# A sum of weight tiles made by accumulating transfers in place of VectorE adds, in a two-block transformer on one core

## The reference, cut to what matters

```
x = x + rmsnorm(m, g[1])
h = rmsnorm(x, g[2])
f = jnp.square(jax.nn.relu(h @ mlp_w1[i])) @ mlp_w2[i]     # (256,2048) @ (2048,8192), then @ (8192,2048)
x = x + rmsnorm(f, g[3])
```

## Time and profile before

| what | value |
|---|---|
| three runs | 2268.59, 2268.76, 2268.84 us (median 2268.76) |
| span of the profiled execution | 2266.9 us |
| granted TensorE clock, mean | 0.999 |
| PE busy | 2255.3 us, 99% of the span |
| DVE busy | 1675.5 us, 74% |
| ACT busy | 1332.9 us, 59% |
| moved by DMA | 542.63 MB, mean 239 GB/s |

### The profile page before, as it was taken

The page is one execution under the profiler, slowest core; times in us unless marked ns, Lnnn a source line. Parts: engine busy times, 40 slices in busy tenths (PEclk is TensorE's granted clock), DMA queues, the critical chain, the costliest instruction groups (busy, mean ns, idle before and its releaser), DMA issues.

```text
span 2266.9 us, 26633 instructions
## 1 busy us (share of the span) xinstructions
PE 2255.3 (99%) x10625; PEld 1873.7 (83%) x10625; DVE 1675.5 (74%) x2025; ACT 1332.9 (59%) x1775; POOL 104.5 (5%) x138
## 2 busy tenths in 40 slices
PE   9999999999999999999999999999999999999998
PEld 7778888888888888888888888888888888888887
DVE  6676864887788788787878788778788685456664
ACT  6455444766666666666666666666666564444443
POOL 0000000000000000000000000000000010000000
PEclk9999999999999999999999999999999999999999
DMA  9454455899998999886578999989888645643343
GB/s 358 167 174 162 164 186 186 289 291 272 287 303 265 277 292 267 283 282 236 219 281 240 287 289 261 285 281 277 270 281 258 240 152 223 244 172 149 148 163 116
DMA packets 77132, 542.63 MB, mean 239 GB/s; under 512 B 8682, under 2 KB 9013, under 8 KB 13968
## 3 DMA queue, kind: packets, MB, share of 16 engines
q1 hardware_dynamic: 61568, 429.58, 50.2%
q0 software_dynamic: 15296, 111.23, 22.7%
q10 hardware_dynamic: 144, 0.12, 0.0%
HBM read 534.60 MB, written 6.29 MB: 239 GB/s over the span
## 4 chain that ended last, share of the span: by engine, by line
PE 98%; DVE 2%; issue 0%; ACT 0%; ACTq 0%; POOLq 0%; POOL 0%
PE P L359 95%; PE P L362 3%; DVE low L626 0%; DVE R_h L614 0%; DVE R_f L611 0%; DVE R_f_r L611 0%; DVE R_g L614 0%; DVE X L614 0%; ACT R_h L502 0%; ACT EV L533 0%; DVE st L614 0%; DVE R_f L708 0%; ACT X L502 0%; DVE X L611 0%; ACTq L2710 0%
## 5 line engine op out<-in xcount | busy, mean ns | idle before, releaser
L626 DVE TENSOR_TENSOR low<-raw,hi 128x1024 fp32r<-128x1024 f32 (+3 forms) x694 | 813.4, 1200 | 290.7 <-ACT hi L507 286.4
L507 ACT ACTIVATE hi<-raw 128x1024 fp32r<-128x1024 f32 (+3 forms) x694 | 704.5, 1040 | 463.5 <-PE P L359 309.5
L359 PE MATMUL P<-hi,R_h 128*128 128x512 f32 (+2 forms) x2944 | 944.2, 392 | 0.6 <-DVE R_h L614 0.6
L359 PE MATMUL P<-hi,R_f_r 128*128 128x512 f32 x2480 | 791.4, 391 | 0.1
L359 PEld LDWEIGHTS P<-hi,R_h 128*128 128x128 f32 x2944 | 552.3, 188 | 116.4 <-issue 5.8
L359 PE MATMUL P<-low,R_h 128*128 128x512 f32 (+2 forms) x1472 | 570.2, 387 | 0.0
L359 PEld LDWEIGHTS P<-hi,R_f_r 128*128 128x128 f32 x2480 | 465.6, 188 | 96.3 <-DVE R_f_r L611 0.3
L359 PE MATMUL P<-low,R_f_r 128*128 128x512 f32 x1240 | 482.5, 389 | 0.0
L626 DVE TENSOR_TENSOR low<-R_f,hi 128x1024 fp32r<-128x1024 f32 x226 | 267.7, 1221 | 82.9 <-ACT hi L507 82.2
L359 PEld LDWEIGHTS P<-low,R_h 128*128 128x128 f32 x1472 | 276.7, 188 | 54.7 <-issue 2.6
L359 PEld LDWEIGHTS P<-low,R_f_r 128*128 128x128 f32 x1240 | 233.0, 188 | 47.1
(11 more groups left out here) (229 smaller groups left out, 1406.2 us busy)
## 6 DMA issues: line engine op xcount, KB each, us to landing
raw<-in_w_d SPq DMA_DIRECT2D x128, 1024.0 KB, 7.2
R_f<-in_w_u POOLq DMA_DIRECT2D x84, 1024.0 KB, 10.5
raw<-in_w_u SPq DMA_DIRECT2D x72, 1024.0 KB, 5.6
raw<-in_w_z SPq DMA_DIRECT2D x45, 1024.0 KB, 4.9
raw<-in_w_i SPq DMA_DIRECT2D x36, 1024.0 KB, 4.9
R_f<-in_w_u SPq DMA_DIRECT2D x28, 1024.0 KB, 6.9
X<-in_w_u SPq DMA_DIRECT2D x28, 1024.0 KB, 8.7
raw<-in_w_mo SPq DMA_DIRECT2D x16, 1024.0 KB, 4.9
```

The costliest lines, as they stand in the source:

```text
L359: return self.e.matmul(o, l, r, start=start, stop=stop, skip_group_check=True)
L507: self.e.activation(hi, raw, ACT.Copy).then_inc(*self.inc("high_made", ("high", k, d)))
L626: self.e.tensor_tensor(low, raw, hi.bitcast(f32), ALU.subtract).then_inc(*self.inc("low_made", *lows))
```

## The change

`third_sum` no longer issues a DVE addition. It issues a `chain_add`: an accumulating transfer on POOL's queue, from the weights in HBM into the chain tile in `X`, which waits for the load of that chain tile (`linked`). The two tiles of `up(3)` are loaded as before, but are now of the kind "load": their landing tiles are given back at their split. Two semaphores are added. `tile_sum` goes.

```
-    def tile_sum(self, o, i, ready, done):
-        self.wait_ge(ready)
-        self.tt(o, o, i, ALU.add, done)
...
-            kept_at = at_["take"] + 9
-
             def third_sum(j):
-                k = kept_at + j
-                landed = None if listing else plan[k][6]
-                done = ("chained", l, e, 4, j)
-                E.tile_sum(m.chain[j + 2], m.raw[(landed or 0) % NL][:, :], [("linked", l, e, j), ("loaded", k)], done)
-                if not listing:
-                    freed[landed] = done
-                    load_ahead()
+                E.chain_add(j + 2, m.chain[j + 2], a[up_w][8 * e + 6 + j], ("linked", l, e, j), ("chained", l, e, 4, j))
...
-            up(3, 1, SH[4], SL[4], s_m[4], plain(b22, "kept"), third, onto=ms[5])
+            up(3, 1, SH[4], SL[4], s_m[4], plain(b22), third, onto=ms[5])
```

More of the change, by code:

```diff
@@ L351 @@
         product = norm_mean = norm_part = norm_whole = norm_root = relu_square = residual = rope = rope_keys = scale = scaled_parts = scores = side_load = side_taps = sine = sine_of = \
-        split_high = split_low = square_sum = store = tile_sum = chain_load = chain_add = combine = operand_sum = times_row = times_row_apart = pads = group_sums = tail_keys = tail_rows = turn = v_times_k = values = warm = y_back = idle
+        split_high = split_low = square_sum = store = chain_load = chain_add = combine = operand_sum = times_row = times_row_apart = pads = group_sums = tail_keys = tail_rows = turn = v_times_k = values = warm = y_back = idle
 class Pe(Engine):
@@ L2684 @@
 SEMAPHORES = (["product_done", "turn_done", "high_made", "act_done", "low_made", "dve_done", "pow_done", "row0", "row1", "stored"]
-              + [f"ring{k}" for k in range(NL + 1)] + [f"link{k}" for k in range(4)] + ["added0", "added1", "gain", "kept", "back0", "back1"] + [f"w{k}" for k in range(4)] + [f"xt{c}" for c in (0, 2, 4, 6, 8, 12)] + [f"x{g}" for g in range(4)] + [f"c{k}" for k in range(17)])
+              + [f"ring{k}" for k in range(NL + 1)] + [f"link{k}" for k in range(4)] + ["added0", "added1", "added2", "added3", "gain", "kept", "back0", "back1"] + [f"w{k}" for k in range(4)] + [f"xt{c}" for c in (0, 2, 4, 6, 8, 12)] + [f"x{g}" for g in range(4)] + [f"c{k}" for k in range(17)])
 def tensor_program(e, counts, mem, a, out, plan, live):
```

## The result

The changed kernel takes 2309.11 us (median of four runs, 2308.50 to 2310.18), the kernel before 2268.77 us in the same job (four runs, 2268.59 to 2268.84). The ratio is 1.0179, 95% interval 1.0165 to 1.0192: 40.3 us slower, where +8 us was forecast and the range ended at 2304 us. The profiled execution has a span of 2306.5 us, 39.6 us above the 2266.9 us of before.

A forecast was written before the change was run, and what follows sets the result against it. PE was taken to bound the 14 rounds, with DMA at 91% as thin cover. 0 (DVE) + 4 (down(3)) + 4 x 1 (the full rounds) = +8 us, so 2277 us, range 2267 to 2304 us.

The forecast's parts named there:

- So this is worth 0: Removing 62.8 us of DVE additions, and issuing the loads of down(4) and down(5) earlier, each gain 0 us.
- the two ends: DMA work of a round after the change: 79.2 us by the moving rates, 86.8 us by q0's account.
- the rival with the engines as the bound: A round lasts as long as its DMA work: +52 us, 2321 us, half where half the losses go; chance 0.16.
- the prediction's own sign for that rival: Rounds above 85 us with PE waiting on several tiles, the sums for up(4) and up(7) among them.
- the second of the three things read against the queue: The pair issued at 737.14, for up(4), lands later, at about 759; about 4 us left, no stall.
- the forecast's own 759: Forecast landing time of the later transfer of the pair issued at 737.14, up from 754.8.
- 0.3 us in the mean: Stall at down(3) per round: load landing in 11.7 us against a limit of 11.4; 4 us over 14 rounds.
- the other end that was kept: Upper case for the load of down(3): 12.1 + 1.2 us against the limit of 11.4, a stall of 1.9 us.
- the slot for this load comes free as before, tied to PE's own pace: At the load of down(3): each round pays its stall anew, nothing is carried over; 14 x 0.3 = 4 us.
- 4 x 1: The four rounds at DMA share 0.94 to 0.95 lose 1 us each, between 0 and +6.1 us.
- start losses: What transfers lose starting on idle DMA engines, 6.5 us a round; most should go with a never-empty queue.
- the moving rates: DMA price per transfer while moving: 2.5 us a load, 4.9 us an addition; 79.2 us a round after the change.

The follow-up runs named there:

- narrow transfers: Changed kernel, but the two new additions of a round move 128 of 2048 columns; 2269.53 us, ratio 1.0003.
- late return: Changed kernel, but the landing tiles of up(3) are given back when down(2) is done on PE; 2310.32 us, ratio 1.0182.
- The narrow last transfer: Changed kernel, but the second addition of the round's last pair, which feeds up(4), moves 128 of 2048 columns; 2286.94 us, ratio 1.0083.
- the other order of the splits: Changed kernel, but both halves of up(4)'s second tile are split before the steps that follow up(7); 2308.60 us, ratio 1.0172.
- first round-ahead kernel: Changed kernel, but the new additions are issued in down(5) of the round before, from round 2 on; 2293.90 us, ratio 1.0114.
- additions behind the load: Changed kernel, but POOL issues the two new additions only when the load of down(3) has landed; 2367.39 us, ratio 1.0432.

## Why the prediction was wrong

The forecast was right on what was removed. "So this is worth 0" for DVE and for the earlier loads stands (narrow transfers 2269.5 us; late return 2310.3 against 2309.1). It was right that the load of down(3) would be late, and on the size of the DMA work: 75.9 us became 83.9 where the two ends were 79.2 and 86.8. The time fell where the rival with the engines as the bound had it (chance 0.16, "from 2290 up"), and the prediction's own sign for that rival came out: rounds above 85 us, with a wait for the sum of up(4) (hardly for up(7)'s, where 0.7 us are lost in all). But the cause is that rival's only in part. The engines are at 0.97 and not full, nearly all waits are at two places, and the share of the engines alone is about 10 us by the steady rounds with the additions a round ahead.

**The step that failed** is the second of the three things read against the queue: "a split needs 2.3 us; about 4 us are left. No stall." The landing itself was forecast well: 759 in the round shown, 21.9 us after 737.14, or 19.6 after the issue at 739.4, against 18.6 measured and 18.8 in the mean. What is wrong is what was put behind it. In the trace before PE starts up(4) at 762.50; at 226.8 ns each, 24 matmuls later, at 767.94, it starts down(6), where the chain of place 2 ends. The chain from landing to there is 9.25 us, and so the landing had to come by 758.7. Read in full, the forecast's own 759 was 0.3 us late and not 4 us early. On top, the last pair is issued behind the splits that wait for the late load of down(3): 5.9 us after PE's start of down(3) (1436.47 less 1430.55), where it was 4.1 (739.4 less 735.29). 18.6 + 1.8 = 20.4 us against 758.7 - 739.4 = 19.3 allowed gives 1.1 us a round, 15.4 in 14 rounds; measured 15.9. That these agree so well is partly luck: it is one round's working, and by round the place lost nothing in the first of each MLP, 5.2 us in the third and 0.4 to 1.5 in the others. The narrow last transfer takes that place's loss away as a whole, and the other order of the splits shows that the chain counts in full.

**A term too small:** down(3), "0.3 us in the mean", 4 us in all. PE loses 1.2 us at the start of the product and 0.15 within it: 19.3 us. The 1.2 can be added up. The landing takes 12.2 us and not 11.7 (0.5), near the other end that was kept (12.1 + 1.2 = 13.3). From landing to PE it is 2.4 us, not the 2.3 of the forecast's working, so the limit in the round shown is 11.3 us and not 11.4 (0.1). And the load is not issued at one fixed lead on PE's start of up(3), as "the slot for this load comes free as before, tied to PE's own pace" has it. That lead is 8.2 us in the round shown, but 7.4 in the first round of each MLP, in both traces, so the limit there is 10.4 us. In five more rounds of the kernel after it is 7.1 to 8.1 where it was 8.2 before. In the mean this is 0.3 us. Sum: 0.3 + 0.5 + 0.1 + 0.3 = 1.2. The first round after shows it: issued at 472.1, landed after 12.2 us, limit 10.4, PE late by 1.8:

```profile
486.72 0.50 PE L359 MATMUL P<-hi,R_f_r 128*128 128x512 f32 x1 [1.62 <-DVE low L626]
```

The loss within the product fits a slow restart (the first matmul after a wait takes 0.50 us on PE and not 0.39). The rows that set the price of the landing were loads with one pair of additions beside them; here two pairs stand in a row, which none of those rows had.

**A term of the wrong kind:** "4 x 1" for the full rounds. Those four (the first three and the ninth) lost 2.6, 2.3, 8.0 and 3.0 us, the ten others 2.4 in the mean; only the third stands out. In it a load of 1 MiB of other data comes on POOL's queue, and the last pair takes 22.2 us to land; no run without that load was made. PE waits up to 3.4 us there, and in the stretch 694 to 699 the granted clock is 0.66, where it was 1.00 ten microseconds earlier at work without a gap. In the piece at 1.2 GHz two matmuls start 0.43 us apart (694.87 and 695.30) instead of 0.227, and so such a wait costs more than itself. The ten steady rounds, which the forecast put at 0 because most of the start losses should go in a queue that is never empty, were not free either. Even at a share of 1.00, with the additions a round ahead, a round lasts 83.5 to 84.1 us where the moving rates give 79.2: of the 6.5 us above the moving rates that were called start losses, more than 4 stay.

In numbers: forecast 0 + 4 + 4 = 8. Measured: down(3) 19.3, up(4) 15.9, elsewhere 4.4: 39.6.

The two rules of the Trainium skill named in the prediction can be judged now. By the Trainium skill, DMA: Bandwidth & Descriptors, "Queues, rings and completion order", each engine alternates between queues that have work. The trace agrees with what the forecast took from it, a load that slows as long as additions last: 12.1 us against 9.5. By the Trainium skill, same page, "Anatomy of one DMA", an addition of 1 MiB would keep the engines busy for an estimated 2.4 us, its bytes at 436 GB/s. The trace doesn't agree: the work of a round rose by 4.0 us for each.

What stays open: how much of the 39.6 us is the engines' sum and how much the due times (about 10 and 30 by the round-ahead kernel, but that one has its loads in another order), and what the other load in the third round has to do with its 8 us. No version here beats the kernel before, and there is little to win for one: PE waited for nothing in these rounds.

## What to carry to other kernels

Relieving an engine that is busy 74% of the time and holds nobody up is worth nothing; look first at what the substitute uses, here DMA engines at 91%. Before transfers are added to a busy queue, write down for each transfer near them its issue, its landing and the latest landing that holds nobody up, and count behind that landing every instruction in order on each engine up to the next product, not just the one that reads it. Where waits are at due times and not at the sum, moving the added transfers moves the wait, and only a place with slack at all landings helps.

## What the runs showed of the hardware

- A load that shares the engines with accumulating transfers hardly gets shorter with half of its bytes: 11.3 us instead of 12.2, where a whole one alone takes 4.9. It has as many packets (128), of 4 KiB instead of 8. That fits engines that take turns by the packet and not by the byte; I didn't test it further.
- One wait of PE of 3.4 us was followed by matmuls at half the clock (0.66 granted over 5 us), and so was one of 2.3 us in the first round-ahead kernel (0.66 over 531.5 to 536.5); the waits of up to 1.6 us at down(3) were not (mean clock of a steady round 1.00). In the kernel with additions behind the load there are 16 waits of 2.2 us and more in the rounds, and the mean clock of the whole run falls from 0.999 to 0.988.
- Eight accumulating transfers a round, with plain loads between, can run the engines at a share of 0.99 to 1.00 with hardly a wait of PE (83.5 to 84.1 us a round). By the rates of the earlier trace rows the same bytes would take 79.2 us, so a queue that is never empty still loses over 4 us a round.
